# The last norm's gains loaded, and four output tiles stored, in pieces of 119, 7 and 2 rows

## The chip, the cores and the metric

The kernel runs on one core of one Trainium2 chip. The metric is the device time of one execution in microseconds (us). The core's engines are called PE (TensorE), DVE (VectorE), ACT (ScalarE), POOL (GpSimd) and SP (SyncE), and 16 DMA engines move data between HBM and the on-chip memory, which has 128 partitions. SP issues the plain transfers of this kernel, POOL the indirect ones.

## The reference

One decoding step of a hybrid layer for 512 prompt tokens and 64 sample tokens, all of width 1024. The first two sub-layers are a token mixer and an attention to memory tokens. The third, an expert retrieval, is most of the time. The last norm makes the outputs `y_prompt` and `y_sample`.

```python
def block(xt):                       # 128 tokens
    ...
    idx = jnp.take_along_axis(cidx, sel, axis=-1)            # 8 heads x 16 experts per token
    gate = jax.nn.softmax(top, axis=-1)
    h = jnp.einsum('td,thkd->thk', xt, u_tab[idx]).astype(jnp.float32)
    a = (jax.nn.gelu(h, approximate=False) * gate).astype(xt.dtype)
    return jnp.einsum('thk,thkd->td', a, v_tab[idx])
...
xp = xp + peer_ffn(rms_norm(xp, g_ffn[l]), *peer_w)
...
y_prompt = rms_norm(xp, g_final)     # x / sqrt(mean(x*x) + eps) * g_final
y_sample = rms_norm(xs, g_final)
```

## The kernel before

The 576 tokens are five tiles: tile 0 holds the 64 sample tokens, tiles 1 to 4 hold 128 prompt tokens each. The residual rows of a tile t stay in `x_res`, as `xr(t)`: one token to a partition, 1024 floats (4 KB) to a row.

The expert retrieval is a loop over 36 blocks of 16 experts, so over 576 steps g. Step g fetches, for each of 128 partitions, one row of `in_peer_uv` (8 KB: the expert's u row and v row) into a slot. POOL issues this gather at L675, after a wait for the matmuls that read the slot's former content (`v_used`). There are up to nine slots from step 278 on. When the gather has landed (`landed`), DVE multiplies the u half with the tokens and sums (L1532), ACT makes the coefficient (L944, L948) and a diagonal matrix from it (L953), and PE multiplies this with the v half into PSUM (L2093, eight matmuls). A step's work on each engine is in order of g, and the rest of the kernel, such as the next tiles' queries and scores, is done in between.

Tiles end one after another. At a tile's end DVE adds the PSUM sums to `xr(t)`, and some blocks later `final(t)` does the last norm: ACT the sum of squares and the root, DVE the reciprocal and, at L1520, the product with the gains `g_fin`, which counts `fin_y` up by one. `final` of tiles 0 to 3 runs in blocks 18, 19, 21 and 29 of the expert loop. Tile 4's norm stands behind the loop, in two halves of 512 columns (L1566 to L1576).

SP's program is one list in order. Its last part, L612 to L630, waits for `l_sc` (the last tile's memory attention), loads `g_final`, broadcast to all partitions, into `g_fin` and counts `ld_ffn`. Then it waits for each tile's `fin_y` and stores the tile, tile 0 to `out_y_s` and the others to `out_y_p`, counting `stored`. The last wait, for all of `stored`, ends the program. The only reader of `g_fin` is DVE's `final` and the last norm behind the loop, and nothing reads what the stores write.

Of the kernel before, what the change touches and what calls it, by code (L numbers as in the profile page):

```python
# [14 lines left out]
P = 128  # L15
D = 1024
KD = D // P
TILES = 5
NTOK = TILES * P
SAMPLES, SAMPLE_LEN = 8, 8  # L20
NS = SAMPLES * SAMPLE_LEN
# [10 lines left out]
SLOT_PHASES = ((0, (9, 8)), (2, (1, 2, 3, 4, 9, 8)), (8, (1, 2, 3, 4, 9)), (14, (3, 4, 9, 1, 2, 5)),  # L32
               (18, (0, 9, 1, 2, 3, 4, 5)), (31, (0, 1, 2, 3, 4, 5, 7, 9)), (74, (0, 1, 2, 3, 4, 5, 7)), (140, (0, 1, 2, 3, 4, 5)), (225, (0, 1, 2, 3, 4, 5, 6)), (278, tuple(range(9))))
WCO_BACK = 200
MKV_PARTS = ((0, 1), (1, 2), (2, 4), (4, 6), (6, 8))
ROW = 2 * D
DIAGS = 6
# [75 lines left out]
def hybrid_step(nc, I, O):  # L113
    ctx = ExitStack()
    with ctx:
# [3 lines left out]
        def sem(name):  # L119
            return ctx.enter_context(nc.semaphore(name))  # L120
# [21 lines left out]
        def v3(ap, a):  # L142
            return ap.rearrange("p (a b) -> p a b", a=a)

        def xr(t):
            return x_res[:, t * D:(t + 1) * D]
# [123 lines left out]
        def qcT(t):  # L270
# [3 lines left out]
        g_fin = R[:, 27392:28416]  # L274
# [43 lines left out]
        warm = sem("warm")  # L318
        ld_mkv = [sem(f"ld_mkv{i}") for i in range(len(MKV_PARTS))]
        ld_gains = sem("ld_gains")  # L320
# [4 lines left out]
        ld_wout, ld_wcq, ld_wco, ld_swa, ld_gating, ld_sk, ld_ffn, ld_rot, ld_late = (  # L325
            sem(n) for n in ("ld_wout", "ld_wcq", "ld_wco", "ld_swa", "ld_gating", "ld_sk", "ld_ffn", "ld_rot", "ld_late"))
# [3 lines left out]
        s_stored, stored, mem_stored = (sem(n) for n in ("s_stored", "stored", "mem_stored"))  # L330
# [59 lines left out]
        def tile_of(b):  # L390

            return (b + 4) // 8
# [93 lines left out]
        def _(sp):  # L486
            def load(dst, src, s):
                sp.dma_start(dst, src).then_inc(s, 16)

            load(gains[:, :], I["gains"][:, :], ld_gains)  # L490
            for i, (a, b) in enumerate(MKV_PARTS):
                k = slice(a, b)
# [116 lines left out]
            load(w_cq2, v3(I["w_cq"][:, :], KD), ld_wcq)  # L609
            sp.wait_ge(v_used, max(g for g in range(WCO_BACK) if slot_of[g] == 7) + 1)  # L610
            load(w_co, I["w_co"][0].rearrange("(k p) n -> p k n", p=P), ld_wco)
# [2 lines left out]
            sp.wait_ge(s_stored, 16 * (2 * SAMPLES + 1))  # L614

            sp.wait_ge(l_sc, TILES)
            load(g_fin, I["g_final"].rearrange("(a d) -> a d", a=1).broadcast_to([P, D]), ld_ffn)
            for t in range(TILES - 1):
                sp.wait_ge(fin_y, t + 1)
                if t == 0:  # L620
                    dst, src = O["y_s"].rearrange("a b d -> (a b) d"), xr(0)[0:NS]
                else:
                    dst, src = O["y_p"][0, (t - 1) * P:t * P], xr(t)
                sp.dma_start(dst, src).then_inc(stored, 16)
            for c in range(2):
                cols = slice(c * 512, (c + 1) * 512)
                sp.wait_ge(fin_y, TILES + c)
                sp.dma_start(O["y_p"][0, (TILES - 2) * P:(TILES - 1) * P, cols], xr(TILES - 1)[:, cols])\
                  .then_inc(stored, 16)
            sp.wait_ge(stored, 16 * (4 + TILES + 1))  # L630


        @block.gpsimd
# [380 lines left out]
        @block.vector  # L1014
        def _(dve):
            chain, _, _ = chain_of(dve, chain_v)

            def gains_of(g, a, b, w):
# [28 lines left out]
            dve.wait_ge(ld_gains, 16)  # L1047
            for i, (a, b) in enumerate(MKV_PARTS):
                part = mem_T[:, a:b]
# [463 lines left out]

            def final(t):

                dve.wait_ge(ld_ffn, 48)
                dve.wait_ge(fin_std, t + 1)
                c = stat[:, 72 + t:73 + t]
                chain(dve.reciprocal(c, stat[:, 64 + t:65 + t]))
                dve.scalar_tensor_tensor(xr(t), xr(t), c, g_fin, ALU.mult, ALU.mult).then_inc(fin_y, 1)  # L1520

            for b in range(BLOCKS):
                t = tile_of(b)
                if starts_tile(b):
                    dve.wait_ge(xn_ready, t + 1)
                for k in range(TOPK):
# [18 lines left out]
                    if k == 12 and b in FINAL_SLOT:  # L1545
                        final(FINAL_SLOT[b])
# [15 lines left out]
            t = TILES - 1  # L1562
# [18 lines left out]
        def _(pe):  # L1581
# [8 lines left out]
            for k in range(KD):  # L1590
                for i, (a, _) in enumerate(MKV_PARTS):
                    if k == a:
                        pe.wait_ge(ld_mkv[i], 32)
                        pe.wait_ge(mg_ready, i + 1)
                for j in range(2):
                    ins = pe.matmul(bank(4 + j), mem_T[:, k, j * P:(j + 1) * P], w_mkv[:, k, :], start=(k == 0),
                                    stop=(k == KD - 1))
                    if k == KD - 1:
                        ins.then_inc(mkv_done, 1)
# [560 lines left out]
```

## Time and profile before

| | us |
|---|---|
| median of three runs | 1706.59 |
| lowest and highest | 1702.78 and 1707.41 |
| the profiled execution's own time | 1704.3 |
| its span, from the first to the last instruction | 1702.5 |

Most times below are those of the profiled execution, from the start of its span. The profile's page gives for each engine its busy share in the whole and in 40 slices. The line `DMA` is the mean busy share of the 16 DMA engines, and `GB/s` is what they moved. A row of DMA queues counts packets: one packet is one contiguous piece of up to some KB that one of the 16 engines moves, and the small packet of 4 bytes with which an engine counts the semaphore when its part of a transfer is done is counted too. The queue q0 is that of POOL's gathers, q1 that of SP's transfers, q8 and q14 fetch instructions.

### The profile page before, as it was taken

What the parts mean: (1) busy time and instruction counts of PE and PEld (TensorE: products, weight loads), DVE (VectorE), ACT (ScalarE), POOL (GpSimd) and SP (SyncE); (2) the same over time, 40 slices, a digit from 0 to 9 for tenths busy, and PEclk for the clock granted to TensorE, in tenths of its full rate; (3) what the DMA queues carried; (4) which work ended last, traced back from release to release, by engine and by line L of the source; (5) the groups of instructions that cost most, each with busy time, mean ns of one, the idle gap of its engine ahead of it and who ended that gap; (6) DMA issues with size and microseconds to landing.
All of it is one profiled execution on the core that took longest, in us unless ns stands there. A gap on an engine that the chain in (4) does not pass through costs nothing.

```text
span 1702.5 us, 21660 instructions
## 1 busy us (share of the span) xinstructions
PE 1300.4 (76%) x7069; PEld 473.6 (28%) x7069; DVE 1165.4 (68%) x2798; ACT 806.5 (47%) x2337; POOL 642.4 (38%) x584
## 2 busy tenths in 40 slices
PE   9998977877889777678777776877667666666766
PEld 4454442433434222123232111212111111111110
DVE  2545648797667676777777777767666677677764
ACT  1524456784444454455555454455444445444443
POOL 0000234433444444444444344434434444444441
PEclk9999999999999888888978887777898878888865
DMA  9526599999999999999999999999999999999995
GB/s 351 172 100 250 220 395 416 414 372 421 421 421 419 417 390 422 421 403 405 421 420 421 421 421 422 421 422 421 420 421 422 421 409 421 422 421 421 422 417 222
DMA packets 97585, 657.88 MB, mean 386 GB/s; under 512 B 12528, under 2 KB 15984, under 8 KB 20784
## 3 DMA queue, kind: packets, MB, share of 16 engines
q0 software_dynamic: 83056, 604.28, 86.0%
q1 hardware_dynamic: 14416, 52.21, 8.1%
q8 instruction: 56, 0.92, 0.2%
q14 instruction: 57, 0.47, 0.1%
HBM read 653.24 MB, written 4.19 MB: 386 GB/s over the span
## 4 chain that ended last, share of the span: by engine, by line
DMA 46%; PE 21%; DVE 12%; ACT 12%; issue 8%; SPq 1%; POOL 1%; ACTq 0%; DVEq 0%; POOLq 0%
DMA R<-in_peer_uv,R 42%; PE ps L2093 10%; DVE R L1532 4%; PE ps L1613 3%; PE ps L1853 2%; ACT L944 2%; ACT R L953 2%; PE ps L1584 2%; ACT R L948 2%; DMA R<-in_mem_prompt 1%; ACT L852 1%; ACT R L944 1%; DVE R L1321 1%; DVE R L1322 1%; DVE R L1324 1%
## 5 line engine op out<-in xcount | busy, mean ns | idle before, releaser
L2093 PE MATMUL ps<-R 64*64 64x512 f32 x4528 | 735.5, 730 | 367.4 <-ACT R L953 349.1
L675 POOL DMA_INDIRECT R<-in_peer_uv,R x566 | 630.0, 1113 | 848.9 <-PE ps L2093 763.8
L1532 DVE CUSTOM_DVE_ANT_0 R<-R 128x1024 f32<-128x1024 f32 x566 | 687.9, 1225 | 373.8 <-DMA R<-in_peer_uv,R 367.0
L944 ACT ACTIVATE R<-R 128x1 f32<-128x1 f32 x576 | 115.8, 201 | 600.2 <-DVE R L1532 580.6
L2093 PEld LDWEIGHTS ps<-R 64*64 64x64 f32 x4528 | 135.5, 150 | 718.0 <-ACT R L953 609.7
L953 ACT ACTIVATE R<-R 128x64 f32<-128x64 f32 x576 | 200.3, 348 | 54.9 <-ACT R L948 1.5
L1853 PE MATMUL ps<-A,R 128*128 128x256 f32 (+1 forms) x640 | 221.1, 467 | 0.7 <-ACT R L829 0.7
L948 ACT ACTIVATE R<-R 128x1 f32<-128x1 f32 x576 | 169.7, 295 | 20.9
L1853 PEld LDWEIGHTS ps<-A,R 128*128 128x128 f32 (+1 forms) x640 | 94.8, 197 | 259.1 <-issue 255.5
L1613 PE MATMUL ps<-A,R 128*128 128x512 f32 (+1 forms) x256 | 101.3, 545 | 0.4 <-ACT R L726 0.4
L1584 PE MATMUL ps<-R 128*128 128x256 f32 (+2 forms) x352 | 80.1, 384 | 0.0
L944 ACT ACT_TABLE_LOAD x61 | 78.3, 1283 | 1.1
L1584 PEld LDWEIGHTS ps<-R 128*128 128x128 f32 x352 | 61.6, 206 | 23.2 <-issue 15.6
L1613 PEld LDWEIGHTS ps<-A,R 128*128 128x128 f32 x256 | 47.0, 190 | 44.3 <-issue 41.4
L675 POOL DMA_INDIRECT x_res<-in_peer_uv,R x10 | 10.0, 998 | 120.1 <-DVE R L1373 107.9
L1532 DVE DVE_READ_ACCUMULATOR2_ANT R<- 128x1 f32 x576 | 47.4, 82 | 0.0
L852 ACT ACT_TABLE_LOAD x34 | 43.6, 1283 | 0.6
L1323 DVE MAX8 R<-R 128x8 f32<-128x128 f32 (+1 forms) x106 | 36.1, 340 | 3.7
L1320 DVE MAX8 R<-R 128x8 f32<-128x128 f32 (+1 forms) x106 | 35.7, 337 | 2.1 <-ACT R L847 0.8
L1324 DVE FIND_INDEX8 R<-R 128x8 uint32<-128x128 f32 (+1 forms) x106 | 35.0, 330 | 0.0
L1321 DVE FIND_INDEX8 R<-R 128x8 uint32<-128x128 f32 (+1 forms) x106 | 35.0, 330 | 0.0
L1322 DVE MATCH_REPLACE8 R<-R 128x128 f32<-128x128 f32 (+1 forms) x106 | 34.0, 321 | 0.0
(302 smaller groups left out, 943.8 us busy)
## 6 DMA issues: line engine op xcount, KB each, us to landing
R<-in_peer_uv,R POOLq DMA_INDIRECT x566
A<-in_w_pq SPq DMA_DIRECT2D x8, 1024.0 KB, 8.9
A<-in_w_in SPq DMA_DIRECT2D x3, 2048.0 KB, 20.3
R<-in_w_out SPq DMA_DIRECT2D x5, 1024.0 KB
x_res<-in_x_prompt SPq DMA_DIRECT2D x6, 512.0 KB, 12.5
R<-in_w_out SPq DMA_DIRECT2D x1, 3072.0 KB
R<-in_x_promptT SPq DMA_DIRECT2D x4, 512.0 KB, 9.0
R<-in_w_cq SPq DMA_DIRECT2D x2, 1024.0 KB, 10.5
```

Of the source, the lines that this page charges most:

```text
L675: pool.indirect_dma_start(slots[slot_of[g]], None, I["peer_uv"][:, :], bass.IndirectOffsetOnAxis(ap=idx[:, b % 4, k:k + 1], axis=0)).then_ ...
L852: act.activation(gate[:, m, :], bestv, ACT.Exp, bias=negtop, accum_out=esum).then_inc(gexp_ready, 1)
L944: act.activation(hgelu[:, b % 2, col], hdot[:, b % 2, col], ACT.Gelu).then_inc(gelu_ready, 1)
L948: act.activation(coef[:, b % 2, col], gate[:, b % 4, col], ACT.Copy, scale=hgelu[:, b % 2, col])\
L953: act.activation(diag[:, g % DIAGS, :], fold[:, 0:HALF], ACT.Copy, scale=coef[:, b % 2, col])\
L1321: chain(dve.max_index(inds[:, 0:8], vals[:, 0:8], values))
L1324: return dve.max_index(inds[:, 8:16], vals[:, 8:16], values)
L1532: dve.tensor_tensor_reduce(u, u, xn(t), 1.0, 0.0, ALU.mult, ALU.add, hdot[:, b % 2, k:k + 1]).then_inc(u_used, 1)
L1584: ins = pe.matmul(out, lhs(k), rhs(k), start=(k == 0), stop=(k == n - 1))
L1613: ins = pe.matmul(out_bank[:, 0:CHUNKS[c][1] - CHUNKS[c][0]], tile_T(t)[:, k, :], w_in[c][:, k, :], start=(k == 0), stop=(k == KD - 1))
L1853: ins = pe.matmul(bank(4)[rows, 0:256], expert_T(t)[:, k, :], w_pq(h)[:, k, :], start=(k == 0), stop=(k == KD - 1))
L2093: ins = pe.matmul(bank(2 * (t % 2) + q)[rows], diag[tokens, g % DIAGS, :], v_rows[slot_of[g]][tokens, c * 512:(c + 1) * 512], start=first, ...
```

## The change

The load of `g_final` and the stores of tiles 1 to 3 are each issued as three transfers in place of one, of partitions 0 to 118, 119 to 125, and 126 and 127. The store of tile 0, with 64 rows, is issued as three of 49, 7 and 8 rows. The waits count the added transfers: `ld_ffn` up to 80 in place of 48, and `stored` by 12 more transfers less the four that they replace. The rows, their addresses and their bytes are the same, and so is the place in SP's list. Tile 4's two stores are left as they were.

```diff
+ROW_CUTS, SAMPLE_CUTS = ((0, 119), (119, 126), (126, 128)), ((0, 49), (49, 56), (56, 64))
...
             sp.wait_ge(l_sc, TILES)
-            load(g_fin, I["g_final"].rearrange("(a d) -> a d", a=1).broadcast_to([P, D]), ld_ffn)
+            for a, b in ROW_CUTS:
+                load(g_fin[a:b], I["g_final"].rearrange("(a d) -> a d", a=1).broadcast_to([b - a, D]), ld_ffn)
             for t in range(TILES - 1):
                 sp.wait_ge(fin_y, t + 1)
                 if t == 0:
-                    dst, src = O["y_s"].rearrange("a b d -> (a b) d"), xr(0)[0:NS]
+                    for a, b in SAMPLE_CUTS:
+                        sp.dma_start(O["y_s"].rearrange("a b d -> (a b) d")[a:b], xr(0)[a:b]).then_inc(stored, 16)
                 else:
-                    dst, src = O["y_p"][0, (t - 1) * P:t * P], xr(t)
-                sp.dma_start(dst, src).then_inc(stored, 16)
+                    for a, b in ROW_CUTS:
+                        sp.dma_start(O["y_p"][0, (t - 1) * P + a:(t - 1) * P + b], xr(t)[a:b]).then_inc(stored, 16)
...
-            sp.wait_ge(stored, 16 * (4 + TILES + 1))
+            sp.wait_ge(stored, 16 * (4 + len(SAMPLE_CUTS) + (TILES - 2) * len(ROW_CUTS) + 2))
...
-                dve.wait_ge(ld_ffn, 48)
+                dve.wait_ge(ld_ffn, 32 + 16 * len(ROW_CUTS))
```

The end of SP's list before, with what each transfer waits for (the numbers behind a name are rows by elements):

```order
L488 DMA R<-in_w_co 128x2x1024 [waits v_used]
L488 DMA R<-in_g_final 128x1024 [waits s_stored,l_sc,mem_stored,stored]
L624 DMA out_y_s<-x_res 64x1024 [waits fin_y]
L624 DMA out_y_p<-x_res 128x1024 [waits fin_y] x3
L628 DMA out_y_p<-x_res 128x512 [waits fin_y] x2
L115 UNCONDITIONAL_BRANCH [waits stored]
```

The same place in SP's list of the changed kernel, up to the first prompt tile:

```order
L489 DMA R<-in_w_co 128x2x1024 [waits v_used]
L489 DMA R<-in_g_final 119x1024 [waits s_stored,l_sc,mem_stored,stored]
L489 DMA R<-in_g_final 7x1024
L489 DMA R<-in_g_final 2x1024
L624 DMA out_y_s<-x_res 49x1024 [waits fin_y]
L624 DMA out_y_s<-x_res 7x1024
L624 DMA out_y_s<-x_res 8x1024
L627 DMA out_y_p<-x_res 119x1024 [waits fin_y]
L627 DMA out_y_p<-x_res 7x1024
L627 DMA out_y_p<-x_res 2x1024
```

Each transfer has become three in a row, and only the first of three waits. The other engines' lists hold the same instructions in the same order as before.

## Rows read from the trace of the kernel before

**Rows 1.** The page: the span, busy engines, the DMA line in 40 slices.

```profile
span 1702.5 us, 21660 instructions
PE 1300.4 (76%) x7069; PEld 473.6 (28%) x7069; DVE 1165.4 (68%) x2798; ACT 806.5 (47%) x2337; POOL 642.4 (38%) x584
...
DMA  9526599999999999999999999999999999999995
GB/s 351 172 100 250 220 395 416 414 372 421 421 421 419 417 390 422 421 403 405 421 420 421 421 421 422 421 422 421 420 421 422 421 409 421 422 421 421 422 417 222
```

**Rows 2.** DVE's waits by releaser, 870 to 1680 us: total, times, longest.

```profile
DVE R L1532 <- DMA R<-in_peer_uv,R: 222.4, 198, 2.2
```

**Rows 3.** The chain that ended last, in order: start, us, what.

```profile
1645.03 17.86 DMA R<-in_peer_uv,R
...
1667.49 17.73 DMA R<-in_peer_uv,R
1685.23 0.04 DVE R L1532
...
1692.45 2.03 PE ps L2093 x8
1694.50 0.68 DVE x_res L1566
...
1698.61 0.75 DVE x_res L1576
```

**Rows 4.** DVE in order of time: the last reductions of the expert loop.

```profile
1680.31 1.23 DVE L1532 CUSTOM_DVE_ANT_0 R<-R 128x1024 f32<-128x1024 f32 x1 [1.25 <-DMA R<-in_peer_uv,R]
...
1685.23 1.23 DVE L1532 CUSTOM_DVE_ANT_0 R<-R 128x1024 f32<-128x1024 f32 x1 [1.23 <-DMA R<-in_peer_uv,R]
...
1687.70 1.22 DVE L1532 CUSTOM_DVE_ANT_0 R<-R 128x1024 f32<-128x1024 f32 x1 [1.23 <-DMA R<-in_peer_uv,R]
...
1690.16 1.22 DVE L1532 CUSTOM_DVE_ANT_0 R<-R 128x1024 f32<-128x1024 f32 x1 [1.23 <-DMA R<-in_peer_uv,R]
```

**Rows 5.** Stretches of the end; last three columns: clock, DMA share, GB/s.

```profile
1678.00:1679.50 1.50, 1.50 (x8) 0.00 (x0) 1.06 (x2) 0.37 (x2) 0.00 (x0) 0.50 0.97 404
1679.50:1680.50 1.00, 0.51 (x8) 0.30 (x8) 0.19 (x1) 0.47 (x2) 0.00 (x0) 0.50 0.63 262
1680.50:1681.80 1.30, 1.30 (x8) 0.00 (x0) 1.04 (x2) 0.20 (x1) 0.00 (x0) 0.50 0.26 101
1681.80:1685.90 4.10, 2.23 (x20) 0.41 (x16) 1.90 (x3) 1.49 (x5) 0.00 (x0) 0.92 0.11 48
1685.90:1690.10 4.20, 2.95 (x17) 0.42 (x16) 1.80 (x4) 1.69 (x6) 0.00 (x0) 0.50 0.06 23
```

**Rows 6.** DMA queues, 870 to 1680 us: packets, MB, share of 16 engines.

```profile
q0 software_dynamic: 46405, 337.92, 100.4%
q1 hardware_dynamic: 512, 1.84, 0.6%
q8 instruction: 23, 0.38, 0.2%
q14 instruction: 27, 0.22, 0.1%
```

**Rows 7.** DVE's groups of instructions, 870 to 1680 us.

```profile
L1532 DVE CUSTOM_DVE_ANT_0 R<-R 128x1024 f32<-128x1024 f32 x320 | 389.3, 1225 | 227.2 <-DMA R<-in_peer_uv,R 222.4 <-issue 2.5 <-DVE R L1324 1.2
```

**Rows 8.** SP's list in order of time, 800 us to the end.

```profile
856.59 0.33 SPq L488 DMA_DIRECT2D R<-in_g_final  x1
994.96 0.49 SPq L624 DMA_DIRECT2D out_y_s<-x_res  x1
1036.21 405.98 SPq L624 DMA_DIRECT2D out_y_p<-x_res  x3
1699.39 0.99 SPq L628 DMA_DIRECT2D out_y_p<-x_res  x2
```

**Rows 9.** DMA queues, 858 to 870 us (the load of the gains).

```profile
q1 hardware_dynamic: 144, 0.52, 10.9%
```

**Rows 10.** DMA queues, 995.5 to 1002 us (the store of tile 0).

```profile
q1 hardware_dynamic: 80, 0.26, 10.0%
```

**Rows 11.** DMA queues, 1445 to 1451 us (the store of tile 3).

```profile
q1 hardware_dynamic: 144, 0.52, 21.4%
```

**Rows 12.** DMA queues, 56.6 to 57.3 us (one 8-row load, 8x8x8).

```profile
q1 hardware_dynamic: 72, 0.00, 5.3%
```

**Rows 13.** DVE in order of time: the first use of the gains.

```profile
993.65 1.28 DVE L1520 SCALAR_TENSOR_TENSOR x_res<-x_res,stat,R 128x1024 f32<-128x1024 f32 x1
```

## Prediction

> **What bounds the kernel now.** The page comes first: from about 200 us to the end the 16 DMA engines are busy in nearly every slice at about 421 GB/s, while PE, the busiest compute engine, has 76% [rows 1]. DVE's waits say the same: from 870 to 1680 us it waits 222.4 us for gathers to land [rows 2]. The chain of waits confirms it, and shows how deep the queue is: the gather issued at 1667.49 us is used 17.73 us later [rows 3], while gathers arrive every 2.47 us at the end (1687.70 to 1690.16) [rows 4]. Seven gathers are in flight. So no single transfer's latency matters, only the sum of work that lies before each DMA engine.
>
> The next question is which of the 16 sets the pace. A gather counts as landed when the last engine has done its share. The end of the loop shows how the 16 stand, since there is nothing left to fetch [rows 5]. Until 1679.5 us all are busy (0.97). In the next 2.3 us the share falls over 0.63 and 0.26 to 0.11, which is two engines of 16 (0.125), until 1685.9 us, and then to 0.06, one engine, until 1690.1. At 1690.16 DVE starts on the last gather. So 14 engines end between about 1679.4 and 1681.8. Their mean: 0.63 x 16 x 1.0 + 0.26 x 16 x 1.3 = 15.5 us of engine time are left after 1679.5, of which 4.6 belong to the two late ones, so 10.9 / 14 = 0.8 us each, mean end 1680.3. One late engine ends at 1685.9, the other, the last, at 1690.1. The kernel is bound by **one engine, which is 8.3 to 10.7 us of work behind the 14**, and the rest ran ahead by the depth of the queue. This lag grows slowly: from 870 to 1680 us the engines took 46405 packets of gathers [rows 6], which at 144 to a gather (128 rows and 16 counts) is 322.3 gathers, while DVE reduced 320 [rows 7]. The last engine fell back by some 2 of 322 gathers against the mean of the others.
>
> **What a row costs.** A 128-row store is 144 packets, 128 rows and 16 counts, and took 21.4% of 16 engines in 6 us [rows 11]: 20.5 us of engine time, 0.160 us a row. The load of the gains gives 0.109 x 16 x 12 / 128 = 0.163 [rows 9], tile 0 with 80 packets (64 rows, 16 counts) 0.100 x 16 x 6.5 / 64 = 0.163 [rows 10]. I take 0.16.
>
> **How the pieces spread.** The 16 counts of a 128- or 64-row transfer say that all 16 engines take part, with 8 or 4 rows each. A transfer of 8 rows (8x8x8) shows 72 packets, which is 64 and only 8 counts: eight engines [rows 12]. So the row count decides how many take part, and all three fit "the largest number up to 16 that divides the rows". No row shows 119 rows. The bounds are all 16 (8 rows at most on one, as before) and one engine (119 rows). I take 7 x 17, the even split that the three rows suggest; 49 gives 7 x 7, 7 gives 7, 8 gives 8, 2 gives 2. The page "DMA: Bandwidth & Descriptors" of the Trainium skill, in "Why a DMA increments its semaphore by 16 and not by 1", states this very rule and adds that the engines used are the lowest-numbered; the trace agrees on 8 against 16 counts, and which engines they are no row shows.
>
> **The sum of work moved.** Call the engines 0 to 15 with the pieces on the lowest. There are four 128-row transfers (the gains, tiles 1 to 3) and tile 0 [rows 8].
> - Before, each engine: 4 x 8 + 4 = 36 rows.
> - Engines 0 and 1 after: 4 x (17 + 1 + 1) + 7 + 1 + 1 = 85 rows, 49 more, +7.84 us.
> - Engines 2 to 6: 4 x 18 + 9 = 81, 45 more, +7.20 us.
> - Engine 7: one row, 35 fewer, -5.60 us. Engines 8 to 15: none, 36 fewer, -5.76 us.
>
> All are 2 x 85 + 5 x 81 + 1 = 576 rows, the same bytes as before. Everything is issued after 856 us, in the DMA-bound stretch, and nothing else in the program hides it or waits for it: the gains have from 857 to the first use at 993.65 us [rows 13], and the stores are read by nobody. SP issues ten transfers more at 0.33 us each [rows 8], in hundreds of us of idle time: nothing. What cover the added rows have is the lag of the last engine: as long as engines 0 to 6 are not the last, their 7 to 8 us cost nothing. With that cover gone they would cost all of it.
>
> **The likeliest case: the late engines are among 7 to 15.** The last engine then ends at 1690.16 - 5.6 = 1684.6, and the second earlier. Engines 0 to 6, of the group with mean end 1680.3, now end at 1680.3 + 7.2 to 7.84 on average and at 1681.8 + 7.84 = 1689.6 at the latest; the last of seven in such a group should be near 1689.0. So the bound passes from one late engine to the seven that got the rows, and the end moves by 0.5 to 2.1 us; I take -1.2. The profiled execution's time is 1704.3, its span 1702.5; it would be 1703.1. The median is 2.3 us above it, and I take the change as it is: 1706.59 - 1.2 = 1705.4.
>
> By count alone nine of sixteen engines are in 7 to 15, a chance of 0.56. I go to 0.75 for the last engine, which is a choice: two engines stand out from 14 that end within 2.4 us, and a steady lag of one of them looks like a duty that is fixed to an engine, and these two are then the pair on which the loads were laid least. In "Latency and other measured facts" the same page of the Trainium skill calls DMA engines 7 and 15 "usually slower than 0-6/8-14 in traces"; that the late engines are exactly two agrees, and their numbers no row here shows. By that rule both lose rows and this case is the whole answer.
>
> **The rivals.**
> - *The last engine is one of 0 to 6: slower.* It gets 7.2 to 7.84 us on top of its lag and still sets the end: 1690.16 + 7.5, so 1714.1. The point from which it decides is simple, which engine is late. For it: seven of sixteen by count. Against: the above. Chance 0.19. The same page's "Rules for kernel authors" asks for a row count that uses all 16 engines; if 119 rows in place of 128 cost what that suggests, it is this time.
> - *Only the second late engine is one of 0 to 6.* It ends at 1685.9 + 7.5 = 1693.4, +3.2 us, 1709.8. Chance 0.13, inside "same".
> - *Everything on all engines anyway*: the pieces are dealt over 16 and nothing moves, 1706.6. The 8 counts of the 8-row load speak against it. Chance 0.04.
> - *The lag was the whole loss: faster.* In an execution with more lag than the profiled one (the slowest is 3.1 us over it), the relief counts up to its full 5.6 us: 1701.0. For it the slack of engines 0 and 1 would have to be 5.6 + 7.84 = 13.4 us. Chance 0.05.
> - *One engine takes all 119 rows.* (4 x 119 + 49 - 36) x 0.16 = 78 us on one engine less at most 10.7 of slack: +68 us, 1774. The even split of 8 rows speaks against it. Chance 0.02.
>
> The likeliest proper keeps 0.57: the 0.75 above less the 0.13 and the 0.05 that share its first condition.
>
> **How the numbers follow.** A difference under 0.3%, 5.1 us, can't be told from no change. Same: 0.57 + 0.13 + 0.04, and 0.01 from the slower case, whose +7.5 us is 0.44% and may be measured as less: 0.75. Faster: 0.05. Slower: 0.19 + 0.02 - 0.01 = 0.20. The range goes from the full relief, 1701.0, up to 1713, which takes in the second engine's case and most of the slower one's lower half. The likeliest case alone would be 1703 to 1708.
>
> **What would show it.** The queue rows of a store should keep their 128 rows but have 16 counts fewer or the same: 7 + 7 + 2 = 16 for a prompt tile, and 7 + 7 + 8 = 22 for tile 0, so 86 packets in place of 80. If tile 0's store shows 112 packets (64 and 3 x 16), all engines took part. A store should take longer from its first to last packet, as 17 rows alternate with 17 gather rows on seven engines. In the stretches of the end the steps 0.125 and 0.06 should be gone in the likeliest case: the share should fall to about 7/16 some 13 us before the last landing, as nine engines finish 5.7 us sooner and seven 7 to 8 us later. If one engine works alone for 8 us as before, or for 15, the slow rival holds. After each store the landings seen by DVE should be late by up to 1.7 us once. The prediction is wrong if the lag is not a property of an engine but moves with the queue, so that relief or load is made up for elsewhere.

## The result, and the profile after

| | before | after |
|---|---|---|
| median, us | 1706.59 (7 runs) | 1715.42 (7 runs) |
| lowest and highest, us | 1700.13 and 1710.94 | 1711.79 and 1717.44 |
| the profiled execution's own time, and its span, us | 1704.3, 1702.5 | 1716.53, 1714.7 |

The change made the kernel slower: the ratio of the times is 1.0062, with a 95% interval from 1.0046 to 1.0079, or +10.6 us of 1706.59 (7.9 to 13.5); the two medians lie 8.8 us apart. The median of 1715.42 is outside the predicted range, 1701 to 1713, and on the side to which 0.20 was given.

The page of the changed kernel, against [rows 1]: instructions, DMA share and GB/s in 40 slices, and the whole of SP's queue.

```profile
span 1714.7 us, 21670 instructions
...
DMA  9426599999999999999999999999999999999995
GB/s 358 161 99 249 209 370 422 420 373 421 421 421 421 416 393 413 421 411 421 421 388 415 421 421 421 405 413 420 420 419 420 418 394 422 417 421 418 416 415 223
...
q1 hardware_dynamic: 14422, 52.21, 8.0%
```

Ten instructions more, the DMA engines as busy as before, and slice 21, in which the gains are loaded, at 388 GB/s in place of 420. From the page alone nothing could be said about the cause. Which engine ends last is read at the end, in the same five stretches as [rows 5], set back from the last landing by the same distances (the last three columns are clock, DMA share and GB/s):

```profile
1690.28:1691.78 1.50, 0.81 (x8) 0.00 (x0) 1.15 (x2) 0.29 (x2) 0.00 (x0) 1.00 0.96 399
1691.78:1692.78 1.00, 0.30 (x4) 0.21 (x8) 0.10 (x1) 0.56 (x2) 0.00 (x0) 0.98 0.53 221
1692.78:1694.08 1.30, 1.30 (x8) 0.00 (x0) 1.13 (x2) 0.13 (x1) 0.00 (x0) 0.50 0.26 101
1694.08:1698.18 4.10, 2.96 (x16) 0.61 (x16) 1.89 (x3) 1.56 (x6) 0.00 (x0) 0.50 0.10 42
1698.18:1702.38 4.20, 3.28 (x20) 0.41 (x16) 1.81 (x4) 1.69 (x6) 0.00 (x0) 0.50 0.06 23
```

The shape is that of before: fourteen engines end 8 to 11 us before the last landing, one some 4 us before it, and one engine works alone to the end. The steps 0.10 and 0.06 are still there, so the two late engines were not relieved.

**Where the time came in.** DVE's reductions are in order of the step, so the same reduction can be found in both traces by counting, and the distance between two of them shows a loss that lies between. One pair stands around the gains load. DVE in the changed kernel, from the reduction before the load to the seventh after it:

```profile
858.00 1.22 DVE L1535 CUSTOM_DVE_ANT_0 R<-R 128x1024 f32<-128x1024 f32 x1
859.96 1.23 DVE L1535 CUSTOM_DVE_ANT_0 R<-R 128x1024 f32<-128x1024 f32 x1 [0.73 <-DMA R<-in_peer_uv,R]
864.37 1.23 DVE L1535 CUSTOM_DVE_ANT_0 R<-R 128x1024 f32<-128x1024 f32 x1 [1.43 <-DMA R<-in_peer_uv,R]
869.76 1.23 DVE L1535 CUSTOM_DVE_ANT_0 R<-R 128x1024 f32<-128x1024 f32 x1 [4.16 <-DMA R<-in_peer_uv,R]
873.50 1.23 DVE L1535 CUSTOM_DVE_ANT_0 R<-R 128x1024 f32<-128x1024 f32 x1 [2.50 <-DMA R<-in_peer_uv,R]
875.99 1.23 DVE L1535 CUSTOM_DVE_ANT_0 R<-R 128x1024 f32<-128x1024 f32 x1 [1.26 <-DMA R<-in_peer_uv,R]
...
880.96 1.22 DVE L1535 CUSTOM_DVE_ANT_0 R<-R 128x1024 f32<-128x1024 f32 x1 [1.25 <-DMA R<-in_peer_uv,R]
```

The same two reductions of the kernel before:

```profile
855.90 1.22 DVE L1532 CUSTOM_DVE_ANT_0 R<-R 128x1024 f32<-128x1024 f32 x1
...
873.82 1.23 DVE L1532 CUSTOM_DVE_ANT_0 R<-R 128x1024 f32<-128x1024 f32 x1 [1.25 <-DMA R<-in_peer_uv,R]
```

22.96 us against 17.92: **5.0 us were lost at the gains load**, and two waits show most of it, 4.16 and 2.50 us where 1.25 is usual. Around the store of tile 1 (issued at 1044.3 us after, 1036.2 before) the sixteenth reduction behind the store stands for the rest. After, then before:

```profile
1046.63 1.23 DVE L1535 CUSTOM_DVE_ANT_0 R<-R 128x1024 f32<-128x1024 f32 x1 [1.20 <-DMA R<-in_peer_uv,R]
...
1089.05 1.23 DVE L1535 CUSTOM_DVE_ANT_0 R<-R 128x1024 f32<-128x1024 f32 x1 [1.25 <-DMA R<-in_peer_uv,R]
```

```profile
1038.52 1.23 DVE L1532 CUSTOM_DVE_ANT_0 R<-R 128x1024 f32<-128x1024 f32 x1 [1.19 <-DMA R<-in_peer_uv,R]
...
1079.49 1.23 DVE L1532 CUSTOM_DVE_ANT_0 R<-R 128x1024 f32<-128x1024 f32 x1 [1.25 <-DMA R<-in_peer_uv,R]
```

42.42 us against 40.97: 1.45 us. Measured in this way tile 0's store cost 0.7 us and those of tiles 1 to 3 1.45, 1.43 and 1.42; between these places the shift stays the same within 0.25 us. From the reduction at 858.00 to the last one at 1702.44 the kernel lost 10.2 us, 5.0 at the load and 5.2 behind it, where the stores are. Another 2.1 us of the 12.2 between the two spans lie before 858 us, where both kernels are the same. The kernels below, the same up to there too, stand between -1.9 and +4.2 us against before at that reduction, so this part says nothing of the change.

The queue rows of the changed kernel, in the stretches of tile 0's store (1002.5 to 1014 us) and of tile 1's (1044 to 1060 us):

```profile
q1 hardware_dynamic: 86, 0.26, 5.7%
...
q1 hardware_dynamic: 144, 0.52, 8.0%
```

86 packets are 64 rows and 22 counts, 7 + 7 + 8. 144 are 128 rows and 16 counts, 7 + 7 + 2. The pieces did spread as predicted.

### The profile page after: what moved, and what is told of

It is laid out like the page before. It is cut to its first block, busy times and chain, and to the rows that moved or that the text cites. A ratio compares the mean times of both kernels' runs of the same rounds, so it can differ in the third digit from the quotient of the medians.

```text
span 1714.7 us, 21670 instructions
## 1 busy us (share of the span) xinstructions
PE 1307.7 (76%) x7069; PEld 476.6 (28%) x7069; DVE 1165.1 (68%) x2798; ACT 806.8 (47%) x2337; POOL 646.1 (38%) x584
## 4 chain that ended last, share of the span: by engine, by line
DMA 44%; PE 23%; DVE 12%; ACT 12%; issue 8%; POOL 2%; ACTq 0%; DVEq 0%; POOLq 0%
DMA R<-in_peer_uv,R 42%; PE ps L2096 9%; PE ps L1616 5%; DVE R L1535 4%; ACT L947 2%; PE ps L1856 2%; ACT R L956 2%; ACT R L951 2%; PE ps L1587 1%; POOL R L678 1%; ACT R L947 1%; ACT L855 1%; DVE R L1324 1%; DVE R L1325 1%; DVE R L1327 1%
```

## The experiments

The shifts below are all worked out as above, against the kernel before: the gains load from the reduction before it to the seventh after it, a store over some sixteen reductions, the extra stores from the reduction at 1501.98 us (before) to the thirtieth after it. In kernels that leave a place unchanged the figure of a store is 0.15 in size at most, and that of the gains load -0.5 to +0.2; only the kernel with more instructions on DVE drifts between these places, and is read in another way. The changed kernel has seven runs and the first three kernels below have twelve each. All others ran once, and their single times scatter as those of the kernel before do (1700.13 to 1710.94 us), so they are judged by the shift inside one trace and not by their time.

### One part of the change at a time

The changed kernel with the stores whole:

```diff
+GAIN_CUTS = ((0, 119), (119, 126), (126, 128))
+ROW_CUTS, SAMPLE_CUTS = ((0, 128),), ((0, 64),)
```

The gains load and the wait for it go by `GAIN_CUTS` in this kernel and in the next.

> Only the gains are loaded in 119, 7 and 2 rows, all stores are whole. Theory A (the last DMA engine is one of the seven that get the rows, and the load in pieces slows the gathers beside it as well): landings 3 to 5 us later from 870 us on and to the end, so +3 to +5 us. Theory B (only the extra rows of the last engine count, 10 to 11 rows at 0.16 us): +1.7 us. Theory C (the loss is in the stores, and the gains' step was chance): 0.

And with the gains load whole:

```diff
+GAIN_CUTS = ((0, 128),)
+ROW_CUTS, SAMPLE_CUTS = ((0, 119), (119, 126), (126, 128)), ((0, 49), (49, 56), (56, 64))
```

> Only the stores are in pieces, the gains are loaded whole. Theory A and B: steps of 1.6 us at each of the three prompt tiles' stores and 0.8 us at tile 0's, +5.6 us in all. Theory C: all of the loss, +9 to +11 us.

| | median, us | before on that chip | ratio, 95% | gains load | tile 0, 1, 2, 3 |
|---|---|---|---|---|---|
| changed kernel | 1715.42 | 1706.59 | 1.0062 (1.0046 to 1.0079) | +5.0 | +0.7, +1.45, +1.43, +1.42 |
| gains only | 1710.13 | 1704.63 | 1.0036 (1.0020 to 1.0052) | +3.5 | 0.0, -0.1, 0.0, -0.1 |
| stores only | 1709.03 | 1704.63 | 1.0035 (1.0021 to 1.0049) | -0.5 | +0.7, +1.43, +1.52, +1.42 |

Both halves cost, each at its own place and nowhere else, and they add up: 1.0036 and 1.0035 to 1.0062 within the intervals. The stores cost about what the ten rows more (five for tile 0) on an engine of the first seven should, 1.4 to 1.5 us where ten rows at 0.16 are 1.6. The gains load costs two to three and a half times that, although it moves as many rows to the same engines as one store; the same load took 3.5 us in one trace and 5.0 in the other, a difference that no run explains. So there are two mechanisms.

### The same three pieces, cut to divide by 16

```diff
-ROW_CUTS, SAMPLE_CUTS = ((0, 119), (119, 126), (126, 128)), ((0, 49), (49, 56), (56, 64))
+ROW_CUTS, SAMPLE_CUTS = ((0, 96), (96, 112), (112, 128)), ((0, 32), (32, 48), (48, 64))
```

> As many transfers as in the change, but of 96, 16 and 16 rows (32, 16 and 16 for tile 0), which all 16 engines share evenly, 8 or 4 rows each as before. Theory A and B (where the rows go is the cost): 0, and the queue rows show 128 rows and 48 counts for a tile. Theory D (three transfers in place of one are the cost, through the counts, the issue or the interleaving): as slow as the change, +9 to +11 us.

DMA queues from 1037 to 1054 us of this kernel, the store of tile 1:

```profile
q1 hardware_dynamic: 176, 0.52, 7.7%
```

176 is 128 rows and 48 counts: all 16 engines in each of the three. The shift at each of the four stores is 0.0 us. So it isn't the number of transfers that costs at the stores, nor the 32 counts more, but the uneven deal of rows. At the gains load 1.3 us stay (19.21 us between the two reductions), though here every engine has its eight rows and nothing was expected. The median is 1708.45 against 1704.63, ratio 1.0020 (1.0004 to 1.0036), which holds the 1.3 us of the load; the interval is too wide to say that there is more.

### What slows the gathers beside the gains load

DMA from 858 to 872 us: GB/s in 40 slices, total packets and mean rate, of the kernel before,

```profile
GB/s 398 421 398 468 421 410 410 421 363 445 421 445 363 421 456 398 363 375 456 480 421 421 421 398 375 421 445 468 421 421 421 398 375 421 468 468 398 421 421 398
DMA packets 877, 5.86 MB, mean 418 GB/s; under 512 B 99, under 2 KB 99, under 8 KB 227
```

of the changed one,

```profile
GB/s 468 375 421 398 421 468 421 339 410 363 281 304 246 398 187 386 211 211 339 281 339 328 257 433 164 386 269 363 257 328 199 398 129 339 257 374 246 269 410 269
DMA packets 687, 4.53 MB, mean 324 GB/s; under 512 B 72, under 2 KB 72, under 8 KB 198
```

and of the one with even pieces:

```profile
GB/s 375 492 398 363 421 316 269 316 351 199 351 199 398 246 258 375 199 316 375 258 316 363 375 410 375 445 445 398 398 421 445 398 421 445 445 398 398 421 445 398
DMA packets 806, 5.12 MB, mean 366 GB/s; under 512 B 118, under 2 KB 118, under 8 KB 246
```

Before, the load runs beside the gathers and the sum stays at 421 GB/s. In pieces, everything that is moved falls to some 300 GB/s for as long as the pieces run, some 10 us, and with even pieces for some 6 us. The stores do nothing of the kind: around tile 1's store the changed kernel has its 422 (1044 to 1060 us). The DMA engines are no less busy beside the pieces; their packets take longer. An 8 KB packet of the gathers that starts between 858 and 872 us takes 0.31 us in the mean in the kernel before, 0.41 in the changed one and 0.35 with even pieces. Two kernels look for the reason. In the first the gains are 128 different rows in HBM in place of one row that all pieces read:

```diff
-                load(g_fin[a:b], I["g_final"].rearrange("(a d) -> a d", a=1).broadcast_to([b - a, D]), ld_ffn)
+                load(g_fin[a:b], I["x_prompt"][0, a:b, :], ld_ffn)
```

> Only the gains' load is in pieces, and it reads 128 different rows (prompt tokens) in place of one row 128 times; the last norm's gains are therefore wrong. If the gathers beside the load were slow because the engines read the same 4 KB of HBM, their packets are at 0.31 us here and the step at 870 us is 1.6 us. If it is the writing side (which partitions an engine writes), the step stays at 3 to 5 us with about 300 GB/s for ten us.

In the second there are three transfers as well, but cut by columns, so that each writes all 128 partitions:

```diff
+            for a, b in ((0, 512), (512, 768), (768, 1024)):
+                load(g_fin[:, a:b], I["g_final"][a:b].rearrange("(a d) -> a d", a=1).broadcast_to([P, b - a]), ld_ffn)
...
-                dve.wait_ge(ld_ffn, 48)
+                dve.wait_ge(ld_ffn, 80)
```

> The kernel before, with the gains loaded in three transfers of all 128 partitions (512, 256 and 256 columns), so three transfers beside the gathers but each engine writes the partitions that it writes in the whole load. If three transfers are what slows the gathers beside the load, their packets take 0.41 to 0.43 us and the landings step by about 1.5 us or more at 870 us. If it is that the pieces of 119 (or 96) rows make engines write partitions other than those of the whole load, the packets stay at 0.31 us and there is no step above 0.4 us.

The same row, 858 to 872 us, of the kernel with different rows in HBM:

```profile
DMA packets 699, 4.57 MB, mean 327 GB/s; under 512 B 78, under 2 KB 78, under 8 KB 206
```

And of that with three column pieces:

```profile
DMA packets 1155, 5.80 MB, mean 414 GB/s; under 512 B 128, under 2 KB 384, under 8 KB 512
```

Different rows don't help (327 GB/s, 0.40 us a packet, +3.1 us at the load, 1705.46 us), and three transfers by columns cost nothing (414 GB/s, 0.32 us, -0.2 us, 1704.1 us against 1705.15). It is neither the source nor the number of transfers. What is left of what was varied is which partitions an engine writes at a time: with 128 rows in one transfer each engine writes its eight, and with 119, 7 and 2, or 96, 16 and 16, it must write others. That is a conclusion by exclusion; no row tells the partitions of an engine. "The descriptor swizzle" in the page "DMA: Bandwidth & Descriptors" of the Trainium skill says that in a 128-partition transfer each engine writes the partitions of one port of its own. If so, a piece sends several engines to ports that the gathers of others are filling, and all of them wait; the rates of these five kernels agree, but no row shows a port, and that ports are the reason was not shown.

### Which engine is the last

Pieces of fewer than 16 rows serve as a probe. After step 500, SP issues 32 extra stores of n rows to a scratch output, n = 6 and 4, later 1, 2 and 3. If a store of n rows takes one row to each of the engines 0 to n-1, each of these gets 32 rows more, some 5.1 us at 0.16 us.

```diff
+            sp.wait_ge(v_used, PROBE_AT)
+            for i in range(PROBE_N):
+                sp.dma_start(probe_out[i], xr(0)[0:PROBE_ROWS]).then_inc(stored, 16)
...
-            sp.wait_ge(stored, 16 * (4 + TILES + 1))
+            sp.wait_ge(stored, 16 * (4 + TILES + 1 + PROBE_N))
```

> The kernel before, with 32 extra stores of 4 rows each into a scratch tensor at about 1505 us, so 32 extra rows (5.1 us) on each of the engines 0 to 3 and nothing on the others. If the last engine is among 0 to 3, the landings step by 5.1 us there and the end is 5 us later. If it is 4 to 6, no step, since engines 0 to 3 have 6 to 8 us of slack by then. If the extra rows cost on whichever engine they are (no single late engine), a step of 5 us as well, with this and with the next probe.

> The same with 32 stores of 6 rows, on the engines 0 to 5. A step of 5.1 us if the last engine is one of 0 to 5, none if it is engine 6 (or one of 7 to 15, which the steps at the stores already speak against). In the tail of the profile the second late engine moves by 5.1 us towards the last if it is among these six.

> The kernel before with 32 extra stores of one row, so 32 extra rows on engine 0 alone. If one late engine sets the pace and it is one of 1 to 3, there is no step of the landings at 1505 us. If it is engine 0, a step of 5 us. If extra rows cost wherever they are, also 5 us; the tail then tells the two apart only by what happens to the other engines, so the 2-row run goes with it.

> The same with 2 rows, on engines 0 and 1. Late engine 1: a step of 5 us here and none with one row. Late engine 2 or 3: no step in either. Late engine 0, or any engine: 5 us in both.

> The kernel before with 32 extra stores of 3 rows at about 1505 us, on engines 0 to 2. One and two rows made no step and four rows one of 5 us, so the last engine is 2 or 3. A step of about 5 us here makes it engine 2, no step engine 3.

DVE in the kernel with four rows, the reduction before the extra stores and the thirtieth after it:

```profile
1505.50 1.22 DVE L1537 CUSTOM_DVE_ANT_0 R<-R 128x1024 f32<-128x1024 f32 x1 [0.43 <-DMA R<-in_peer_uv,R]
...
1586.53 1.23 DVE L1537 CUSTOM_DVE_ANT_0 R<-R 128x1024 f32<-128x1024 f32 x1 [0.25 <-DMA R<-in_peer_uv,R]
```

And in that with three:

```profile
1505.42 1.23 DVE L1537 CUSTOM_DVE_ANT_0 R<-R 128x1024 f32<-128x1024 f32 x1 [0.45 <-DMA R<-in_peer_uv,R]
...
1580.94 1.23 DVE L1537 CUSTOM_DVE_ANT_0 R<-R 128x1024 f32<-128x1024 f32 x1 [0.21 <-DMA R<-in_peer_uv,R]
```

| rows of each extra store | time, us | before, same chip | shift at the stores |
|---|---|---|---|
| 1 | 1704.01 | 1704.61 | 0.0 |
| 2 | 1703.24 | 1704.61 | -0.1 |
| 3 | 1707.72 | 1710.36 | 0.0 |
| 4 | 1712.86 | 1705.15 | +5.5 |
| 6 | 1708.07 | 1705.15 | +4.8 |

81.03 us against 75.52: with the fourth row, and not with the third, the kernel gets slower by the price of 32 rows. **The last engine is the fourth of the 16, engine 3** if they are used from the lowest, as the numbers of engines here always mean. That 32 rows cost 4.8 to 5.5 us gives 0.15 to 0.17 us a row. The end tells the rest. The last four stretches (from 10.7 to 0.1 us before the last landing) with one row,

```profile
1679.48:1680.48 1.00, 0.38 (x4) 0.21 (x8) 0.18 (x1) 0.47 (x2) 0.00 (x0) 1.00 0.80 336
1680.48:1681.78 1.30, 0.71 (x8) 0.00 (x0) 1.05 (x2) 0.20 (x1) 0.00 (x0) 1.00 0.38 151
1681.78:1685.88 4.10, 2.83 (x12) 0.61 (x16) 1.90 (x3) 1.49 (x5) 0.00 (x0) 0.59 0.12 50
1685.88:1690.08 4.20, 3.23 (x20) 0.41 (x16) 1.80 (x4) 1.69 (x6) 0.00 (x0) 0.58 0.06 23
```

and the last two of them with two:

```profile
1680.71:1684.81 4.10, 2.25 (x20) 0.42 (x16) 1.89 (x3) 1.53 (x6) 0.00 (x0) 0.92 0.15 64
1684.81:1689.01 4.20, 2.97 (x19) 0.41 (x16) 1.81 (x4) 1.69 (x6) 0.00 (x0) 0.50 0.11 45
```

With one row the first two of these stretches hold 0.80 x 16 x 1.0 + 0.38 x 16 x 1.3 = 20.7 us of engine time, where [rows 5] gives 15.5: the 5.1 us of 32 rows lie on one of the fourteen, and move nothing else. With two rows a second engine works nearly to the end (0.11 in place of 0.06). The second row moved the second late engine by all of its 4 us lead, so that is engine 1. With three rows it stands there too (0.11). With four and six the last two shares are 0.10 and 0.11, then 0.06, as before: both late engines got the rows, so the distance between them stays, and not the move of the second that was expected for six. For the two late engines these runs so show that the engines of a smaller piece are among those of a larger one. Both are among the seven that the change loads.

### What makes these two late

The profile counts 57 packets of 8 KB in q14, which fetch instructions. If each engine's fetches always go through the same DMA engine, that is a fixed duty. Four instructions more to a step on ACT, or on DVE, from step 300 on, should then push one late engine back and not the other. The first two kernels had the line marked - below, the two after them the line marked +.

```diff
                 if g >= 300:
                     for _ in range(4):
-                        act.nop()
+                        act.sem_inc(warm, 1)
```

> The kernel before with four NoOp instructions more on ACT in each step from 300 on (1104 in all). If the last engine is late because it also serves ACT's instruction fetches, the packets of q14 rise by some 8 of 57 and the last engine falls back by some 5 us more, landings and end 4 to 6 us later. If it serves DVE's, only the second late engine moves, towards the last, and the end stays within 1 us. If lateness has nothing to do with fetches, neither moves.

> The same 1104 NoOp instructions on DVE. The mirror: if the last engine serves DVE's fetches the end is 4 to 6 us later here and not in the ACT run; if it serves ACT's, the second late engine moves here. No move in either speaks against fetches as the cause.

These two, with the line marked -, say nothing: the page still counts 21660 instructions and 57 packets, so the empty instructions were not in the program. Their times, 1704.82 and 1703.19 us beside 1710.36, are within the scatter of the kernel before. The two that followed count a semaphore up in place of them, 1104 instructions more on ACT, and 1102 on DVE:

> The kernel before with four semaphore counts more on ACT in each step from 300 on: 1104 instructions of 64 bytes, 8.6 packets of 8 KB more on q14. If engine 3 is last because ACT's instructions are fetched through it, the landings drift later by some 0.7 us for each such packet, 5 to 6 us by the end, and the end is as much later. If it serves DVE's, the end stays within 1 us. If lateness has nothing to do with fetches, the end and the second late engine both stay.

> The same 1104 counts on DVE. If ACT's fetches go through engine 3 and DVE's through engine 1, the end stays within 1 us and the second late engine moves 2 to 4 us towards the last. If DVE's go through engine 3, the end is 3 to 6 us later. No move in either kernel speaks against fetches as the cause.

The fetch queue in the page, with more on ACT, and then with more on DVE:

```profile
q14 instruction: 65, 0.53, 0.1%
```

```profile
q14 instruction: 66, 0.54, 0.1%
```

The last two stretches before the last landing, with more on ACT:

```profile
1684.34:1688.44 4.10, 1.92 (x16) 0.42 (x16) 1.89 (x3) 1.49 (x5) 0.00 (x0) 1.00 0.12 52
1688.44:1692.64 4.20, 1.99 (x16) 0.31 (x16) 1.81 (x4) 1.69 (x6) 0.00 (x0) 0.74 0.10 43
```

And the last four with more on DVE:

```profile
1687.39:1688.39 1.00, 0.49 (x8) 0.31 (x8) 0.18 (x1) 0.48 (x2) 0.00 (x0) 0.50 0.20 82
1688.39:1689.69 1.30, 1.30 (x8) 0.00 (x0) 1.05 (x2) 0.20 (x1) 0.00 (x0) 0.50 0.14 44
1689.69:1693.79 4.10, 2.92 (x20) 0.51 (x16) 1.89 (x3) 1.49 (x5) 0.00 (x0) 0.73 0.06 26
1693.79:1697.99 4.20, 2.35 (x16) 0.41 (x16) 1.81 (x4) 1.69 (x6) 0.00 (x0) 0.68 0.06 23
```

With more on ACT the second late engine works nearly to the end (0.10), and from the reduction before the gains load to the last the kernel loses nothing (-0.1 us, where the kernels with one, two and three rows have -0.7 to -0.2; 1706.84 us beside 1710.95). With more on DVE one engine is alone for over 8 us (0.06 twice), and between the same two reductions (855.13 and 1698.05 us) the kernel takes 8.7 us longer, with nine more packets of 8 KB in q14. It took 1712.19 us beside 1710.95, and the distance within one trace is the better measure.

DVE's busy time stays at 1165 us, but this does not clear DVE itself, since the busy time leaves semaphore counts out. Where DVE has other work between two reductions and sets the pace, they are 3.50 us apart with the four counts (1290.90 to 1294.40 us), and 2.99 before. What the fetches cost is seen where DVE has nothing else to do and only waits for gathers. DVE in the same kernel:

```profile
1679.79 1.23 DVE L1535 CUSTOM_DVE_ANT_0 R<-R 128x1024 f32<-128x1024 f32 x1 [1.25 <-DMA R<-in_peer_uv,R]
1683.24 1.22 DVE L1535 CUSTOM_DVE_ANT_0 R<-R 128x1024 f32<-128x1024 f32 x1 [2.21 <-DMA R<-in_peer_uv,R]
1685.73 1.23 DVE L1535 CUSTOM_DVE_ANT_0 R<-R 128x1024 f32<-128x1024 f32 x1 [1.25 <-DMA R<-in_peer_uv,R]
```

and the fetch queue from 1681 to 1682 us:

```profile
q14 instruction: 1, 0.01, 2.0%
```

Where DVE only waits, its reductions are 2.48 us apart. The one at 1683.24 us, 1.7 us after the start of a fetch packet (1681.5), is 3.45 us behind its forerunner. From 1000 us on this trace has nine such distances of 3.42 to 3.46 us where DVE only waits, each 1.7 to 3.6 us after the start of a packet of q14, and there is no other above 3 us. From the reduction at 1639.12 us to the last, with two such packets and where the kernel before has none, 1.9 us are lost. The packets that the kernel with more on ACT has more (at 1033.2, 1108.4 and 1519.6 us, for example) are followed by the usual 2.47 to 2.50 us; only towards the end, when the second late engine has all but lost its lead, do packets of ACT cost something (2.70 and 3.09 us behind those at 1595.6 and 1673.0 us). So each fetch packet of DVE costs the kernel about 1 us, and nine more at this price are the 8.7 us, while the packet itself mostly takes 0.31 to 0.34 us; what the rest is no row shows. DVE's fetches go through the last DMA engine and ACT's through the second late one, the other way round than the first guess in the expectations. In the kernel before, eleven of the packets between 1019.7 and 1621 us follow each other every 56 to 64 us, and where DVE only waits, the landing behind such a one is late in the same way (3.45 us at 1205.4 and at 1565.1, for example). Eleven at 1 us are as much as the last engine's whole lag; that nothing else adds to it was not shown.

## Why the prediction was wrong

- *One DMA engine sets the pace, 8 to 11 us behind 14 others.* Right. 32 rows on engines 0 to 2 cost nothing, and the same rows with engine 3 among them cost their full price.
- *0.16 us a row.* Right: 0.15 to 0.17 from the extra stores.
- *The spread 7 x 17, 7, 2 and 7 x 7, 7, 8.* Right, by 16 and 22 counts, and by the extra stores the two late engines are among the few that take the rows each time.
- *The ten transfers more cost nothing to issue, and "nothing else in the program hides it or waits for it".* Right: with even pieces, as many transfers, each store shifts the landings by 0.0 us.
- *"The likeliest case: the late engines are among 7 to 15", 0.75.* **This is the step that failed.** The last is engine 3 and the second engine 1, so they got 45 and 49 rows more where this case takes some 36 from each, and between the same two reductions the landings came 10.2 us later where 1.2 us earlier was forecast. The reason I gave for going from the 0.56 of plain counting to 0.75, that a fixed duty would be laid on the least used engines, had no row behind it. The fixed duty was a fair reading, and the fetches bear it out; its place was a guess. What the Trainium skill says in "Latency and other measured facts" of "DMA: Bandwidth & Descriptors", that engines 7 and 15 are usually slower, does not hold in this kernel, if the engines are numbered as above. The range followed the same step: it ended at 1713, below the 1714.1 that the slow rival had for itself, and the measured 1715.42 is 1.3 us from that rival.
- *The slow rival's price, +7.2 for an engine of 2 to 6.* Right in kind, mis-sized in one term. Its 45 rows are 35 of the stores (5 + 3 x 10), 5.6 us, where 5.0 to 5.2 were measured, and 10 of the gains load, 1.6 us, where 3.1 to 5.0 were measured, since the load in pieces slows every gather beside it. That a transfer could slow others beyond its own bytes stood in none of the cases. In place of the 7.2 us of this term the trace shows 10.2. That the rival's 1714.1 still comes near the median is luck in part: the medians, with their scatter, moved by 8.8 us only.
- *"Nine engines finish 5.7 us sooner."* Wrong, without effect on the time: with some 36 rows fewer, while the last engine had 45 more, they ended as long before the last as in the kernel before [rows 5]. That fits a lead limited by how many gathers are issued ahead, so that a relieved engine only waits longer for the next one; no run varied that number. Engines 0, 2, 4, 5 and 6 kept their distance to the last for a simpler reason: it took the same 45 rows as they (engine 0 took four more).
- *"After each store the landings seen by DVE should be late by up to 1.7 us once."* Right: 1.4 at tiles 1 to 3.

## What to carry to other kernels

In a kernel bound by DMA, count rows per DMA engine and not bytes: a transfer whose row count has no large divisor up to 16 lays its rows on few engines, and if the one that is already last is among them the kernel pays each of them in full, while on the others they are free as long as their lead lasts. The engine that is last can be found with small extra stores of one, two, three rows and so on. If a load into partitions has to be cut, columns were the better cut here, with all 128 partitions in each piece; cut by rows it slowed all traffic beside it even where every engine had the same number of rows.

## What the runs showed of the hardware that was not expected

- A load cut by rows into the on-chip memory lowers the rate of all DMA traffic from 418 GB/s to 324 (119, 7 and 2 rows) or 366 (96, 16 and 16) as a mean over 14 us. Stores in the same pieces don't (422).
- Instruction fetches have fixed DMA engines: more instructions on DVE made the last engine later, more on ACT the second. 1102 instructions more on DVE came with nine packets more and 8.7 us, about 1 us a packet, and the same on ACT cost nothing. "Instruction fetch mechanics" in the page "Runtime: NRT & Kernel Launch" of the Trainium skill says that a refill brings 256 instructions in 16 KiB and is mostly hidden. The bytes of an instruction agree (1102 instructions are 69 KiB by it, and nine packets more of 8 KB were counted), though the packets here hold 8 KB and not 16; and hidden it is not where the fetching DMA engine is the bound.
